# First per-layer embedding computed by token: factors on ScalarE, normalised rows turned back by products

## The chip, the cores and the metric

The kernel runs on one core of one Trainium2 chip. The metric is device time in microseconds (us) of one launch, the median of several runs; lower is better. The core's engines are TensorE (PE: matrix products; PEld: its weight loads), VectorE (DVE), ScalarE (ACT), GpSimd (POOL) and SyncE (SP, which here only issues weight loads).

## The reference

One sequence of 256 tokens with 1024 channels passes a first block (token mixer and a convolutional feed-forward part) and then a second block of two layers. Each layer of the second block is a mixer (a short convolution in layer 0, differential attention in layer 1), a feed-forward part and a per-layer embedding. Only the embedding of layer 0 and what touches it matters here:

```
def per_layer_embed(x, p_i, g_pre, w_gate, w_proj, g_post):
    gate = sigmoid(rms_norm(x, g_pre) @ w_gate)          # 256x1024 @ 1024x1024
    return rms_norm(gate * (p_i @ w_proj), g_post)       # 256x256 @ 256x1024
x = x + per_layer_embed(x, p[0], ...)                    # layer 0, then layer 1:
k, v = split(rms_norm(x, g_kv) @ w_kv);  q = rms_norm(x, g_pre_mix[1]) @ w_q
```

rms_norm divides each token by the root of the mean of its squares over the 1024 channels. All is float32.

## The kernel before, in words

**Layout.** The state x lies channel-major: eight chunks of 128 channels (partitions) by 256 tokens. To keep float32 accuracy with the fast product format, each operand is split into a high part (rounded) and a low part (the rest), and each product is done three times: high x high, low x high, high x low. Weights stream through a ring of three slots in blocks of 128x2048: SP loads a block into raw, ScalarE rounds it to w_hi (`split`, `ahead`, line 1662), VectorE subtracts to get w_lo (L2473), TensorE uses it and counts it in block_used. SP loads block n when the low part of block n-3 is done; ScalarE may round block n when TensorE has used block n-3.

**Order.** Each engine has one instruction queue, written out by hand; engines wait for each other on semaphores. Blocks n to n+3 below are the gate's four blocks, n+4 and n+5 the first two of attention (keys).

**Layer 0's embedding, by channel** (`ffn_and_ple`, L1475, on TensorE; L2257 on ScalarE; L3353 on VectorE). The projection p @ w_proj is done in two halves: the first half early, in `first_post` (L773), while the norm of the mixer's result is awaited; the second half (`late_proj`) when the feed-forward part ends, with the mean of its squares (`mean_of_y`) between. Both go by `proj_rows`, with channels as output partitions. The gate product x @ w_gate follows as x's chunks are updated (`high`, `part`, `channel_rows`): two blocks by parts, then the third whole, then `mean_of_x` (the mean of x's squares, from VectorE's sum folded at L2505), then the fourth, each bank of PSUM counted in bank_summed as it is finished. VectorE multiplies each bank by x's factor (L3382, L3384), ScalarE takes the sigmoid in place (L2281), VectorE multiplies by the projection (L3390, L3392), ScalarE squares (L2335), VectorE squares the last two (L3403), TensorE sums the squares over channels against ones (`mean_of_products`, L796) and fills with eight products of zeros (`keep_busy`, L708), ScalarE makes the factor (`rstd_y`, L1847), and VectorE scales, adds to x and makes attention's first operand (`add_post`, `led_chunks`, L3080). The first two chunks' high parts are made ahead of x's update (`early`, L3087).

**Layer 1's embedding, by token** (`last_layer`, L809; `last_products`, L2294 and L3424). Here tokens are the output partitions: bank b holds tokens 128 t to 128 t + 127 (t = b // 2) and half the channels (b % 2). x's factor is then one number a partition, so that ScalarE applies it as the scale of the sigmoid (L2302), squares with the sum over channels read as a by-product (L2311), and no mean on TensorE is needed for the products. The last bank is done in two halves (`last_quarter`, `half_sigmoid`). The mean of x's squares by token (`mean_by_token`, L891) stands inside the fourth block's second quarter. GpSimd makes factors by a power (L556, L558) for x and for the first tile; ScalarE makes the second tile's by Ln and Exp (L2329, L2330).

**Behind the embedding** the attention blocks start: `columns_by_chunk(5, ...)` (L615) does the first two key blocks chunk by chunk of x, 96 products, as the chunks' high and low parts come; the low part of the second block's weights is wanted from chunk 1 on (`second`, L627).

Of the kernel before, what the change touches and what calls it, by code (L numbers as in the profile page):

```python
# [16 lines left out]
P = 128  # L17
TOK = 256
# [91 lines left out]
SUMS_OF_ROW = [3, 3, 4, 4, 3, 4, 4, 5]  # L110
LED = (3, 5, 6)
SIX_FIRST = (6, 0, 1, 2, 3, 4, 5, 7)
SQUARES_OF_POST = [5, 5, 3, 5, 5, 4]
SUMS_OF_POST = [2, 2, 0, 2, 2, 4]
POST_BANK = (5, 4, 4, 5, 4)
GATE_BANK = (5, 0, 1, 2)
LAST_GATE_BANK = (6, 0, 1, 2)
TURN_BANK = (3, 5, 6, 7)
LAST_HALF_BANK = (2, 4)

# [6 lines left out]
def build(nc, weights, small_in, x_in, masks_in, ident_in, channel_in, row_in, w_gk_in, p_in, table_in,  # L127
# [4 lines left out]
    with ExitStack() as ctx:  # L132
# [311 lines left out]
        token_ms, minus_half = att_stat[1][:, 0:4], att_stat[1][:, 4:8]  # L444

# [67 lines left out]
        def _(pool):  # L513
# [34 lines left out]
            pool.dma_start(p_tok, p_in[1]).then_inc(sem("p_loaded"), 16)  # L548
            pool.wait_ge(sem("logits_read"), 8)
# [8 lines left out]
            pool.tensor_tensor(norm_r[:, 0:1], norm_bias[:, 0:1], minus_half[:, 0:1], ALU.pow).then_inc(sem("y_rstd"), 1)  # L558
# [3 lines left out]
        def _(pe):  # L562
# [52 lines left out]
            def columns_by_chunk(p, n0, banks, operand):  # L615
# [5 lines left out]
                if p in LED:  # L621
                    order = high[0:4] + low[0:1] + high[4:5] + low[1:4] + high[5:6] + low[4:6] + high[6:7] + low[6:7] + high[7:8] + low[7:8]
                for k, lo in order:
                    pe.wait_ge(lo_chunk if lo else hi_chunk, chunk_at(p, k) if lo else hi_at(p, k))
                    for j, bank in enumerate(banks):
                        slot = (n0 + j) % RING
                        second = j == 1 and k == 0 and not lo  # L627
                        if k == 0 and j == 0 and not lo:
                            block_ready(n0)
                        elif second:  # L630
                            pe.wait_ge(hi_ready, n0 + 2)
                        elif k == 1 and j == 0 and not lo:
                            pe.wait_ge(lo_ready, n0 + 2)
                            for f in range(2):
                                add(PS[:, banks[1], f * TOK:(f + 1) * TOK], w_lo[:, (n0 + 1) % RING, f * P:f * P + P], a_hi[:, 0, :])
# [72 lines left out]
            def keep_busy(n, bank):  # L708

                for _ in range(n):  # L710
                    add(PS[:, bank, :], zeros_r[:, 0:P], zeros_r[:, :], True, True)
# [35 lines left out]
            def proj_rows(layer, c, kk, w, first):  # L747


                o = PS[:, 6 + c // 2 % 2, (c % 2) * TOK:(c % 2 + 1) * TOK]  # L750
                ws_hi, ws_lo = w[0][:, kk, (c % 4) * P:(c % 4 + 1) * P], w[1][:, kk, (c % 4) * P:(c % 4 + 1) * P]
                p_hi, p_lo = p_parts(layer)
                add(o, ws_hi, p_hi[:, kk, :], first and kk == 0)
                add(o, ws_hi, p_lo[:, kk, :])
# [3000 lines left out]
```

## Time and profile before

| | |
|---|---|
| median of 3 runs | 1010.14 us (1009.93 to 1010.57) |
| the profiled execution | 1009.94 us, span 1008.1 us |
| granted TensorE clock, mean | 0.998 |
| TensorE busy | 997.1 us |
| VectorE busy | 848.4 us |
| ScalarE busy | 620.5 us |
| GpSimd busy | 9.5 us |

A timeline row tells the start in us from the span's start, the time of the row, the engine, the line of the kernel, the operation with output<-inputs, shape and count, and in square brackets the engine's idle time before it and who ended it. Rows of products have modelled ends: the time from one row's start to the next is what a product takes of the queue. A float32 product that is not in the fast format makes two records.

### The profile page before, as it was taken

The numbers are of one execution on the slowest core, as the hardware profiler recorded it, in microseconds if no ns is written. First come the engines' busy times: TensorE is split into PE (matmuls) and PEld (weight loads), VectorE is DVE, ScalarE is ACT, GpSimd is POOL, SyncE is SP. The second block draws the span as 40 slices with busy tenths as digits, with TensorE's granted clock in tenths as the row PEclk, the third lists the DMA queues.
The fourth block names the chain that finished last, engine by engine and source line by source line (L and its number), as shares of the span: only waits on it lengthen the run. The fifth ranks groups of instructions, "written<-read, shape, count | busy, mean of one in ns | idle before, by whom it ended". The sixth has DMA issues, their size and how long they took to land.

```text
span 1008.1 us, 20874 instructions
## 1 busy us (share of the span) xinstructions
PE 997.1 (99%) x8362; PEld 936.5 (93%) x8362; DVE 848.4 (84%) x1226; ACT 620.5 (62%) x858; POOL 9.5 (1%) x21
## 2 busy tenths in 40 slices
PE   8999999999999999999999999999999999999997
PEld 7999999999999998899999999999999999999996
DVE  5974896899988878879999888899776899988887
ACT  6754565657565655466666555775677676555575
POOL 0000001000000000001000000000000000000000
PEclk9999999999999999999999999999999999999999
DMA  9533315455655545566566554444444355655541
GB/s 330 179 124 97 126 44 201 165 192 187 208 190 184 196 143 204 180 235 210 199 209 209 174 203 171 165 165 170 165 147 152 126 204 205 212 178 196 184 150 42
DMA packets 26786, 177.04 MB, mean 176 GB/s; under 512 B 3261, under 2 KB 3541, under 8 KB 6368
## 3 DMA queue, kind: packets, MB, share of 16 engines
q1 hardware_dynamic: 25616, 171.31, 49.2%
q0 software_dynamic: 1104, 4.78, 1.6%
q8 instruction: 50, 0.82, 0.3%
q14 instruction: 16, 0.13, 0.0%
HBM read 175.02 MB, written 2.63 MB: 176 GB/s over the span
## 4 chain that ended last, share of the span: by engine, by line
PE 91%; DVE 4%; DMA 2%; ACT 2%; issue 1%; SPq 0%; DVEq 0%
PE PS L613 78%; PE PS L564 12%; DMA arena<-masks_in 1%; DVE w_lo L2473 1%; DMA raw<-weights 1%; DVE arena L2614 1%; DVE h_store L2486 0%; PE PS L1567 0%; DVE x L3158 0%; ACT w_hi L1662 0%; DVE arena L3390 0%; DVE arena L3152 0%; PE PS L935 0%; PE PS L903 0%; ACT arena L2043 0%
## 5 line engine op out<-in xcount | busy, mean ns | idle before, releaser
L613 PE MATMUL PS<-h_store,w_hi 128*128 128x256 f32 (+1 forms) x1840 | 475.5, 338 | 1.4 <-DVE w_lo L2528 1.2
L2473 DVE TENSOR_TENSOR w_lo<-raw,w_hi 128x2048 fp32r<-128x2048 f32 x152 | 347.9, 2290 | 50.6 <-ACT w_hi L1662 45.5
L613 PE MATMUL PS<-h_store,w_lo 128*128 128x256 f32 (+1 forms) x1400 | 365.4, 281 | 0.1
L1662 ACT ACTIVATE w_hi<-raw 128x2048 fp32r<-128x2048 f32 x154 | 294.2, 1911 | 82.6 <-PE PS L613 70.2
L613 PEld LDWEIGHTS PS<-h_store,w_hi 128*128 128x128 f32 x1840 | 303.6, 187 | 40.6 <-DVE w_lo L2528 1.7
L613 PEld LDWEIGHTS PS<-h_store,w_lo 128*128 128x128 f32 (+1 forms) x1400 | 253.2, 188 | 0.5 <-DVE h_store L3087 0.3
L613 PE MATMUL PS<-act_hi,w_hi 128*128 128x256 f32 x688 | 191.1, 280 | 0.2 <-DVE act_hi L3087 0.2
L613 PE MATMUL PS<-act_hi,w_lo 128*128 128x256 f32 x688 | 190.7, 279 | 0.1
L613 PE MATMUL PS<-act_lo,w_hi 128*128 128x256 f32 x688 | 187.6, 279 | 0.0
L613 PEld LDWEIGHTS PS<-act_hi,w_hi 128*128 128x128 f32 x688 | 129.3, 188 | 1.6 <-DVE act_hi L3087 0.6
L613 PEld LDWEIGHTS PS<-act_hi,w_lo 128*128 128x128 f32 x688 | 129.3, 188 | 0.3 <-DVE act_hi L3087 0.3
L613 PEld LDWEIGHTS PS<-act_lo,w_hi 128*128 128x128 f32 x688 | 127.5, 188 | 0.0
L2156 ACT ACTIVATE arena<-PS 128x512 f32<-128x512 f32 x51 | 30.2, 592 | 88.1 <-PE PS L613 88.1
L2148 ACT ACTIVATE arena<-arena,channel 128x256 f32<-128x256 f32 x132 | 63.6, 530 | 13.6 <-DVE arena L3235 12.4
L613 PE MATMUL PS<-w_hi,h_store 128*128 128x256 f32 (+1 forms) x368 | 71.3, 301 | 0.0
L3212 DVE SCALAR_TENSOR_TENSOR arena<-arena,channel 128x254 f32<-128x254 f32 x132 | 57.9, 480 | 7.6 <-DVE arena L3208 0.3
L613 PEld LDWEIGHTS PS<-w_hi,h_store 128*128 128x128 f32 x368 | 56.2, 188 | 2.9 <-ACT w_hi L1776 0.4
L3208 DVE SCALAR_TENSOR_TENSOR arena<-arena,channel 128x255 f32<-128x255 f32 x132 | 57.7, 479 | 1.0 <-ACT arena L2148 0.9
L3233 DVE TENSOR_TENSOR arena<-PS,arena 128x512 f32<-128x512 f32 x51 | 35.0, 686 | 20.9 <-ACT arena L2156 20.9
L613 PE MATMUL PS<-w_lo,h_store 128*128 128x256 f32 (+1 forms) x184 | 45.8, 296 | 0.4 <-DVE w_lo L2473 0.4
L564 PE MATMUL PS<-h_store,w_hi 128*128 128x256 f32 x256 | 45.4, 279 | 0.0
L564 PE MATMUL PS<-arena 64*64 64x64 f32 (+8 forms) x1356 | 41.5, 224 | 0.0
(405 smaller groups left out, 1147.1 us busy)
## 6 DMA issues: line engine op xcount, KB each, us to landing
raw<-weights SPq DMA_DIRECT2D x155, 1024.0 KB, 5.0
raw<-weights SPq DMA_DIRECT2D x12, 256.0 KB, 4.0
arena<-masks_in SPq DMA_DIRECT2D x1, 1600.0 KB, 12.2
bias_by_key<-bias_by_distance POOLq DMA_DIRECT2D x1, 1536.0 KB, 8.5
x<-x_in SPq DMA_DIRECT2D x4, 256.0 KB, 4.4
raw<-weights SPq DMA_DIRECT2D x2, 512.0 KB, 8.3
arena<-weights POOLq DMA_DIRECT2D x2, 512.0 KB, 6.1
arena<-bias_by_key POOLq DMA_DIRECT2D x1, 1024.0 KB, 6.6
```

The costliest lines, as they stand in the source:

```text
L564: return pe.matmul(o, lhs, rhs, start=start, stop=stop)
L613: return pe.matmul(o, lhs, rhs, start=start, stop=stop, skip_group_check=True)
L1662: act.activation(w_hi[:, slot, :], raw[:, slot, :], ACT.Copy).then_inc(hi_ready, 1)
L2148: ins = act.activation(dst[:, c, :], src[:, c, :], ACT.Identity, scale=w, bias=b)
L2156: act.activation(low, PS[:, bank:bank + 2, TOK:512], ACT.Copy).then_inc(sem("low_copied"), 1)
L2473: tt(w_lo[:, slot, :], raw[:, slot, :], w_hi[:, slot, :].bitcast(F), ALU.subtract).then_inc(lo_ready, 1)
L2614: mark(stt(dst, PS[:, bank_of_block(n), f * TOK:(f + 1) * TOK - d], ch("gdn_conv", (3 - d) * 6 + 2 * s + f), dst, ALU.mult, ALU.add))
L3208: stt(y[:, c, 1:TOK], src[:, c, 0:TOK - 1], channel[:, bass.ds(col(1) + c, 1)], y[:, c, 1:TOK], ALU.mult, ALU.add).then_inc(ready[0], 1)
L3212: ins = stt(y[:, c, 2:TOK], src[:, c, 0:TOK - 2], channel[:, bass.ds(col(0) + c, 1)], y[:, c, 2:TOK], ALU.mult, ALU.add)
L3233: tt(z, PS[:, bank:bank + 2, 0:TOK], low, ALU.add).then_inc(sem("parts_added"), 1)
```

## The change

Layer 0's embedding is computed like layer 1's, by token:

- TensorE: the projection goes by `proj_tokens` in both layers, and `last_layer` becomes `embedding(layer, p, q)` for both. In layer 0 the mean by token stands behind the third gate block's first quarter, and the last bank's products of the third block are done with that block (`halves(4, 6)`), so that only those of the fourth remain at the end. `mean_of_products` and `proj_rows` go. Six products of zeros follow, then the new part: the products g, which lie by token, must come back by channel. `scale_and_turn` multiplies a 128x128 piece of g with a diagonal matrix of the token factors (`rate_rows`), which scales and turns it in one float32 product: eight for the first tile of tokens, then four of the second, and the last four between the first attention products (`turn_second_tile`).
- ScalarE: `gated_products` for both layers (token factor as the sigmoid's scale); two more copies of the late projection; at the end the second tile's factor and its diagonal matrix (a scaled copy of ident).
- GpSimd: the first tile's factor by a power and its diagonal matrix (a product of ident with a column).
- VectorE: no reading with a factor, no scaling; `add_turned` updates x straight from the turned banks. The low part of the second attention block is made in two halves, the second within `add_turned`; `columns_by_chunk(5, ...)` wants it four chunks later (`late = 4`). In both layers the first tile's mean stands before the third product.

```diff
@@ GpSimd
+            link(pool.memset(minus_half, -0.5))
+            pool.wait_ge(sem("y_sum"), y_sum(2, 1))
+            link(pool.tensor_tensor(norm_r[:, 0:1], norm_bias[:, 0:1], minus_half[:, 0:1], ALU.pow))
+            pool.tensor_scalar(rate_rows[0], ident[:, :], norm_r[:, 0:1], None, ALU.mult).then_inc(sem("first_rate"), 1)
             pool.wait_ge(sem("logits_read"), 8)
@@ TensorE, columns_by_chunk
+                late = 4 if p == 5 else 1
                 for k, lo in order:
+                    if p == 5 and k in (1, 2) and not lo:
+                        turn_second_tile(range(2 * k + 2, 2 * k + 4))
...
-                        second = j == 1 and k == 0 and not lo
+                        second = j == 1 and k < late and not lo
@@ TensorE, first_post
-                proj_rows(0, 0, 0, early_proj, True)
+                proj_tokens(0, 0, 6, 0, early_proj)
                 mean_of_y(0)
-                proj_rows(0, 0, 1, early_proj, True)
-                proj_rows(0, 1, 0, early_proj, False)
+                proj_tokens(0, 0, 6, 1, early_proj).then_inc(sem("proj_half"), 1)
+                proj_tokens(0, 1, 7, 0, early_proj)
                 biases_by_head()
...
+                proj_tokens(0, 1, 7, 1, early_proj).then_inc(sem("proj_half"), 1)
@@ TensorE, embedding
+            def scale_and_turn(c, t):
+
+                return mm(turned(c)[:, t * P:(t + 1) * P], by_quarter[:, 2 * t + c // 4, (c % 4) * P:(c % 4 + 1) * P], rate_rows[t])
+
+            def turn_second_tile(chunks):
+
+                for c in chunks:
+                    done = scale_and_turn(c, 1)
+                    if c in (0, 1, 3, 5, 7):
+                        done.then_inc(sem("y_scaled"), 1)
...
                 for b in range(3):
                     gate(2, b)
+                    if layer == 0 and b == 0:
+                        mean_by_token()
+                if layer == 0:
+                    halves(4, 6, False).then_inc(block_used, 1)
...
                 gate(3, 0).then_inc(bank_summed, 1)
-                gate(3, 1, mean_by_token).then_inc(bank_summed, 1)
+                gate(3, 1, mean_by_token if layer else None).then_inc(bank_summed, 1)
                 gate(3, 2).then_inc(bank_summed, 1)
...
+                halves(4 if layer else 6, KC, True)
+                if layer == 0:
+                    keep_busy(6, 5).then_inc(block_used, 1)
+                    pe.wait_ge(sem("first_rate"), 1)
+                    pe.wait_ge(sem("gate_sigmoid"), 3)
+                    for c in range(KC):
+                        last = scale_and_turn(c, 0)
+                    last.then_inc(sem("y_ms"), 1)
+                    pe.wait_ge(sem("y_rstd"), q + 2)
+                    turn_second_tile(range(4))
@@ ScalarE, gated_products
                 gate_sigmoid(0)
                 gate_sigmoid(1)
                 square(0)
-                gate_sigmoid(2)
-                square(1)
+                if layer:
+                    gate_sigmoid(2)
+                    square(1)
+                else:
+                    square(1)
+                    gate_sigmoid(2)
                 half_sigmoid(0)
                 square(2)
...
                 half_sigmoid(1)
                 act.preload_act_table_set(TABLES)
...
                 link(act.activation(r, sum_of_squares[:, 4:5], ACT.Ln, bias=norm_bias[:, 1:2]))
-                act.activation(r, r, ACT.Exp, scale=-0.5).then_inc(sem("y_rstd"), 1)
+                if layer:
+                    act.activation(r, r, ACT.Exp, scale=-0.5).then_inc(sem("y_rstd"), 1)
+                else:
+                    link(act.activation(r, r, ACT.Exp, scale=-0.5))
+                    act.activation(rate_rows[1], ident[:, :], ACT.Copy, scale=r).then_inc(sem("y_rstd"), 1)
@@ VectorE, add_turned (new)
+                early(0, first_gain, first_x)
+                early(1, second_gain, second_x)
+                update(2)
+                update(3)
+                update(0)
+                update(4)
+                lo(0, 3)
+                between()
+                update(1)
...
@@ VectorE, ffn_and_ple
+                gated_products(layer, z, q + 1)
                 if layer == 0:
...
+                    half_lo(n + 5, 0)
+                    add_turned(p + 1, q + 1, lambda: half_lo(n + 5, 1))
```

## Rows read from the trace of the kernel before

**Rows 1.** The page, part 1: busy time of each engine, share of the span, instructions.

```profile
PE 997.1 (99%) x8362; PEld 936.5 (93%) x8362; DVE 848.4 (84%) x1226; ACT 620.5 (62%) x858; POOL 9.5 (1%) x21
```

**Rows 2.** Windows: engines' busy us (instructions), granted clock, DMA share and GB/s.

```profile
640.00:668.00 28.00, 28.00 (x230) 27.57 (x230) 26.64 (x42) 19.94 (x31) 0.00 (x0) 1.00 0.53 184
668.00:674.00 6.00, 5.63 (x24) 3.99 (x23) 5.79 (x12) 5.06 (x8) 0.00 (x0) 1.00 0.14 33
```

**Rows 3.** Timeline of TensorE around the first embedding.

```profile
640.17 0.28 PE L613 MATMUL PS<-first_p_hi,w_hi 128*128 128x256 f32 x1
640.29 0.28 PE L613 MATMUL PS<-first_p_lo,w_hi 128*128 128x256 f32 x1
...
667.52 2.05 PE L613 MATMUL PS<-xn,ones 128*128 128x256 f32 x8
...
673.78 0.39 PE L613 MATMUL PS<-act_hi,w_hi 128*128 128x256 f32 x1 [0.16 <-DVE act_hi L3087]
...
685.55 2.04 PE L613 MATMUL PS<-h_store,w_hi 128*128 128x256 f32 x16
```

**Rows 4.** Timeline of TensorE in the last embedding.

```profile
972.29 0.39 PE L613 MATMUL PS<-w_hi,act_hi 128*128 128x512 f32 x1
...
989.12 0.61 PE L613 MATMUL PS<-w_hi,h_store 128*128 128x512 f32 x2
...
990.48 0.61 PE L613 MATMUL PS<-w_hi,h_store 128*128 128x512 f32 x2
```

**Rows 5.** Timeline of TensorE, first product of the first feed-forward part of the second block.

```profile
456.03 0.28 PE L613 MATMUL PS<-h_store,w_hi 128*128 128x256 f32 x1
```

**Rows 6.** Timeline of VectorE: the fold of the sum of squares.

```profile
657.77 0.43 DVE L2505 TENSOR_TENSOR arena<-arena 128x256 f32<-128x256 f32 x1
```

**Rows 7.** Timeline of ScalarE in the last embedding.

```profile
995.82 1.26 ACT L2302 ACTIVATE arena<-PS,arena 128x512 f32<-128x512 f32 x2 [4.57 <-POOL arena L556]
...
1000.17 0.62 ACT L2311 ACTIVATE xn<-arena 128x512 f32<-128x512 f32 x1
...
1000.83 0.42 ACT L2323 ACTIVATE xn<-arena 128x256 f32<-128x256 f32 x1
...
1001.25 0.46 ACT L2306 ACTIVATE arena<-PS,arena 128x256 f32<-128x256 f32 x1
1001.73 1.28 ACT L2326 ACT_TABLE_LOAD   x1
1003.02 0.29 ACT L2329 ACTIVATE arena<-arena 128x1 f32<-128x1 f32 x1
1003.35 0.20 ACT L2330 ACTIVATE arena<-arena 128x1 f32<-128x1 f32 x1
```

**Rows 8.** Timeline of VectorE in the last embedding.

```profile
999.05 0.69 DVE L3431 TENSOR_TENSOR arena<-arena 128x512 f32<-128x512 f32 x1
...
1001.74 0.43 DVE L3435 TENSOR_TENSOR arena<-arena 128x256 f32<-128x256 f32 x1
```

**Rows 9.** Timeline of TensorE: float32 products of 256 and 128 columns.

```profile
723.65 1.47 PE L613 MATMUL PS<-arena 128*128 128x256 f32 x8
```

**Rows 10.** Timeline of VectorE: the first attention operand.

```profile
673.24 0.48 DVE L3087 SCALAR_TENSOR_TENSOR act_hi<-arena 128x256 fp32r<-128x256 f32 x1
```

**Rows 11.** Groups by line of GpSimd: operation, shape, count, busy us, mean ns, idle time.

```profile
L556 POOL TENSOR_TENSOR arena<-arena 128x4 f32<-128x4 f32 x1 | 1.1, 1052 | 224.8 <-DVE arena L3458 224.8
...
L558 POOL TENSOR_TENSOR arena<-arena 128x1 f32<-128x1 f32 x1 | 0.9, 926 | 4.2 <-DVE arena L3448 4.2
...
L523 POOL MEMSET ones<- 128x128 f32 x1 | 0.2, 209 | 0.0
```

**Rows 12.** The page's DMA issues (part 6), and ScalarE's timeline at the fifth attention block.

```profile
raw<-weights SPq DMA_DIRECT2D x155, 1024.0 KB, 5.0
...
691.13 1.90 ACT L1662 ACTIVATE w_hi<-raw 128x2048 fp32r<-128x2048 f32 x1
```

**Rows 13.** Instructions of line 2281: the sigmoid in place, without a factor.

```profile
L2281 ACT ACTIVATE arena<-arena x5: 399/632/632, 665.2 to 668.6; 128x512 f32<-128x512 f32 x3, 128x256 f32<-128x256 f32 x2
```

More of the change, by code:

```diff
@@ L444, in build, with turned @@
         token_ms, minus_half = att_stat[1][:, 0:4], att_stat[1][:, 4:8]
+        rate_rows = [r_x2[:, t * P:(t + 1) * P] for t in range(TT)]
+        def turned(c):
+            bank, at = TURNED_AT[c]
+            return PS[:, bank, at:at + TOK]
         def hi_at(p, c):
@@ L1491, in ffn_and_ple @@
-                last.then_inc(block_used, 1)
-                n = STEP[f"ple_gate{layer}"]
-                def part(j, k, cs, a, w, first=False):
-                    for c in cs:
-                        at = k % 2 * D + c * P
-                        o = PS[:, GATE_BANK[c // 2], (c % 2) * TOK:(c % 2 + 1) * TOK]
-                        last = add(o, w[:, (n + j) % RING, at:at + P], a[:, k, :], first and c % 2 == 0)
-                    return last
-                def high(k, cs, first=False):
-                    part(0, k, cs, h_hi, w_hi, first)
-                    part(0, k, cs, h_hi, w_lo)
@@ L2275, in ffn_and_ple, with gated_products @@
+                for b in (1, 3):
+                    act.activation(by_quarter[:, b, :], PS[:, TURN_BANK[b], :], ACT.Copy).then_inc(sem("proj_copied"), 1)
+                if layer == 0:
+                    ahead(n + 2)
+                    first_operand(5, 2)
+                    rstd_x(p + 1, 3, r_x[:, TOK:TOK + 4])
                 act.preload_act_table_set("sigmoid_and_others")
+                gated_products(layer, p, q + 1)
+            def gated_products(layer, p, q):
                 z = (s_gate, hidden, y_gate, y_up)
-                def sigmoid(part):
-                    act.wait_ge(sem("ple_z"), part + 1)
-                    v = flat(z[part]) if part < 3 else z[3][:, part - 3, :]
-                    act.activation(v, v, ACT.Sigmoid).then_inc(sem("gate_sigmoid"), 1)
@@ L2301, in gate_sigmoid @@
                     at = TOK + 2 * (b // 2)
-                    act.activation(flat(z[b]), PS[:, LAST_GATE_BANK[b], :], ACT.Sigmoid, scale=r_x[:, at:at + 1]).then_inc(sem("gate_sigmoid"), 1)
+                    act.activation(flat(z[b]), PS[:, GATE_BANK[b], :], ACT.Sigmoid, scale=r_x[:, at:at + 1]).then_inc(sem("gate_sigmoid"), 1)
                 def half_sigmoid(half):
-                    act.wait_ge(bank_summed, bank_sum(7, 4 + half))
+                    act.wait_ge(bank_summed, bank_sum(row, 4 + half))
```

316 lines of the change are left out of this document (112 added, 204 removed).

## The prediction, made before the changed kernel was built

> **What bounds the kernel now.** I read the page first, then the windows around the first embedding, then each engine's timeline there. TensorE is busy 99% of the span [rows 1]. So an edit is worth what it does to TensorE's own order, and other engines count only where TensorE waits for them. The windows show where it does [rows 2]: from 640 to 668 us it never waits, and from 668 to 674 us it has 5.63 busy us of 6, part of which is keep_busy, eight products of zeros. The fixed points are in its timeline [rows 3]: the embedding starts at 640.17, the last gate product's slot ends at 667.52, the first attention product starts at 673.78, and the 96 products of the first two attention blocks end at 685.55. The six us from 667.52 to 673.78 hold a serial chain: read, sigmoid, product, squares, their mean on TensorE, norm on ScalarE, scaling, first operand. From 673.78 on, 96 products at the 0.117 us between neighbouring rows, 640.17 and 640.29, would take 11.25 us; they take 11.77.
>
> The last embedding already has the form that the first is given, so much of the new stage has rows to read. It starts at 972.29, its third gate block's first quarter ends at 989.12, and a quarter block (six products of 512 columns) takes 990.48 - 989.12 = 1.36 us [rows 4].
>
> **The projection and the first two gate blocks.** On the new time line the third block's first quarter ends at 640.17 + (989.12 - 972.29) = 657.00; fewer, wider products are in that figure. The early projection in front of the first feed-forward part goes from 24 products of 256 columns to 12 of 512, the same columns. Its mean starts 3 x 0.117 = 0.35 us later, behind three wide products, and so does the norm; but the wide products behind the mean still last until about 456.03, where TensorE turns to the next operand now [rows 5]. I take 0, and up to 0.35 for the range.
>
> **The mean behind the first quarter: a wait that the change adds.** The mean needs VectorE's folded sum of squares: folded at 657.77 for 0.43 us, so there at 658.20 and not earlier, with no idle time shown before it [rows 6]. TensorE comes at 657.00 and stands until about 658.26: 1.26 us, with all other gate products queued behind. Today the mean stands behind the whole third block, past 661, and waits for nothing. This is the largest single loss. Then come the mean by token (two float32 products of at most 0.22 each, 0.4), five quarter blocks at 1.36, and 24 half products of 256 columns at 0.12, half of them before the fourth block, half behind it: 2.88. The sum is 658.26 + 0.4 + 6.80 + 2.88 = 668.34, against 667.52: the gates end 0.8 later.
>
> **ScalarE and VectorE up to the second tile's factor.** Two copies out of PSUM are added to ScalarE before the token factors; it is idle for 8 us between 640 and 668 [rows 2], and the sigmoids can't start before the first bank sum at 664.2. They cost 0. The second bank sum comes at 658.26 + 0.4 + 2.72 + 1.44 + 2.72 = 665.54, and ScalarE follows some 0.2 behind a product's slot, at 665.75. From there on ScalarE and VectorE alternate, by the last embedding's rows [rows 7, 8]. Sigmoid 1 takes 1.26/2 = 0.63, VectorE's product 0.69, two semaphores 0.1: square 1 starts at 667.17. A square with its sum read takes 1000.83 - 1000.17 = 0.66: sigmoid 2 at 667.83. Again 0.63, 0.69 and 0.1: square 2 at 669.25, the half square at 669.91. It takes 0.42, the last half sigmoid 0.48, the table load 1.29, Ln 0.33, Exp 0.20: Ln starts at 672.10, the factor is there at 672.63. VectorE's half product, 0.43, its reduction and mean, as short, lie beside the table load. So ScalarE's queue sets the end, and the gates' last sums (668.34) are no longer on it. The new row of factors is a copy of 128x128 with no row: between Exp's 0.20 of one column and the 0.48 of 256 columns. I take 0.35, in the middle, so that TensorE starts the second tile at 673.05.
>
> **Turned products.** These are float32 products with 128 columns. Eight records of such work (two products of 256 and two of 128 columns, so six times 128) take 1.47 us with their tail [rows 9]: 0.22 each without it. The first is there 0.45 after its start, at 673.5. VectorE's first operand takes 0.48 [rows 10], and the first attention product starts at about 674.1, against 673.78. So squares of VectorE, eight means of products and a scaling go, and the copy, the turn and the added wait take their place.
>
> **The first tile and GpSimd.** Square 1 ends near 667.9; VectorE's mean and GpSimd's power, 0.93 [rows 11], bring it to 669.1. Then GpSimd multiplies ident by the factor, 128x128, which no row shows. The nearest row is the 128x128 memset, 0.21; the steepest reading is the power's slope, (1.05 - 0.93)/3 = 0.042 us a column, 5.4 us for 128. I take 0.4: a plain product is nearer the memset. TensorE fills until about 669.7, then turns eight chunks in 8 x 0.22 = 1.8 us, to 671.5, and waits 1.5 us for the second tile anyway. So the GpSimd product costs nothing below about 2.1 us. Queued behind its wait are only the loads of the next projection and of the last gains, which wait for the end of the attention heads anyway. The Trainium skill ("GPSIMD Engine Reference", section 3.1) gives an elementwise operation there 1.8 to 2.6 cycles an element and two software hops; an estimate from that page is 0.2 to 0.5 us, and no run here shows it yet.
>
> **The attention blocks.** The last four chunks of the second tile are turned between attention products: 4 x 0.22 = 0.88 us of TensorE, which has 0.52 us of waits to give there. 674.1 + 0.1 + 11.25 + 0.88 = 686.3 against 685.55. VectorE loses its scalings. The low half of the second attention block moves from before the norm into two pieces; the order of products now lets four chunks pass before it is wanted: 24 high and 4 low products and four turns behind 674.2, at 678.4. VectorE gets there after seven operations of some 0.4 and the piece's own 1.2, at 677.6. SP's next load waits for that low part and starts about 5 us later; it lands in 5.0 us, at about 682.7, and ScalarE comes to round it only at 691.13, behind x's factor [rows 12]. Hidden; without that cover it would cost 1 to 3 us.
>
> **Sum.** 686.3 - 685.55 = 0.75 later, and behind it TensorE is as full as before. In the last embedding only VectorE's mean moves ahead of a product, with slack on both sides: 0. The profiled execution took 1009.94 us with a span of 1008.1; the median of the runs is 1010.14, 0.2 above it. I forecast 1010.14 + 0.75 = 1010.9 us.
>
> The token factor as ScalarE's scale: a sigmoid of 512 columns in place, without a factor, takes 0.632 us [rows 13]; with a column of factors it takes 0.63 [rows 7]. The sum takes the factor as free. The Trainium skill ("ScalarE: Activation LUTs", on what ACT_TABLE_LOAD and ACTIVATE cost) says that each [128,1] pointer operand adds about 93 ns, which speaks against this change: by that page the chain's sigmoids and squares would be up to 0.4 us longer, and the time 1011.3. The trace does not agree, unless reading PSUM directly gives it back.
>
> **The rivals.** (a) Faster: TensorE doesn't wait at the mean, as VectorE folds earlier once nothing is read into it, and the turns run at the 0.117 of a product of 256 columns. For it: ScalarE's chain then starts 1.26 earlier. Against: VectorE has no idle time before the fold, and float32 is slower in [rows 9]. It gives 1010.9 - 1.26 - 0.4 - 0.8 (the chunks' waits all covered) = 1008.4 at most. Chance 0.12. (b) Slower: GpSimd's 128x128 product. From 2.1 us on it decides. At the slope's 5.4 the first tile's factors are there at 674.5, turned by 676.3, and the second tile starts then instead of at 673.05: 3.2 us, 1014.1. For it: no row has the form; against: the memset. Chance 0.1. (c) Slower by the clock: TensorE would stand 1.3 us at the mean and 1.5 us before the second tile. The granted clock is 1.00, its 2.4 GHz level, in both windows [rows 2], also where it waits now. At 1.2 GHz every us of its work costs another; three such us give 1014. Chance 0.05. (d) The chain is longer by 1 to 1.8 us than rows of another stage say (more semaphores, a slower copy): 1012.3. Chance 0.1. (e) The forecast, 1009.2 to 1012.0: 0.63.
>
> **How the numbers follow.** A measurement of this kernel tells about 0.2%, 2.0 us, from no change. Faster by more needs most of (a): 0.1. Slower by more takes (b), (c) and half of (d): 0.2. The rest is within: 0.7. The range goes down to the wait absent and cheap turns, 1008.6, and up to (d)'s end, 1012.7; the far ends of (b) and (c) are left out.
>
> **What the profile would show.** Right: TensorE idle for over 1 us before the mean by token, released by VectorE's fold; the gates ending 0.8 later; the row of factors on ScalarE releasing the second tile near 673; the first attention product near 674.1; its blocks ending near 686.3. Wrong: no wait at the mean, turns under 0.15 us, a GpSimd product over 2 us, a granted clock below 1.00 after 657, or the first feed-forward part starting late.

## The result and the profile after

| | before | after |
|---|---|---|
| median, same chip | 1010.17 us (22 runs) | 1011.81 us (22 runs) |
| ratio to before | | 1.0014, 95% interval 1.0008 to 1.0019 |
| profiled execution | 1009.94 us, span 1008.1 | 1013.26 us, span 1011.2 |

The forecast was 1010.9 us: no change that a measurement tells, some 0.75 us slower by its sum. The medians differ by 1.64 us, the ratio of the runs is 1.0014, or 1.4 us (0.8 to 1.9). That lies inside the range and within the 0.2%. But with 22 runs of each kernel the interval is clear of 1: the slowdown is small and real, and about twice the forecast one.

The profiled execution of after is the longest of its 22. So I compare stages, not ends, each from a fixed row to a fixed row of TensorE:

| stage, us | before | after |
|---|---|---|
| first product of the first embedding, to the end of the 96 attention products | 640.17 to 685.55: 45.38 | 641.84 to 688.41: 46.57 |
| from there to the last embedding's first product | 286.74 | 286.58 |
| last embedding, to the end of the span | 972.29 to 1008.1: 35.81 | 974.99 to 1011.2: 36.21 |

The first embedding adds 1.19 us. The last seems to add 0.40, but the span's end is printed to 0.1 us only. Counted to the start of VectorE's last three operations it is 0.36 (these rows are shown below). The stretch between takes 0.16 less. Together that is 1.4 of the 3.1 us by which the spans differ; the other 1.67 lie before the first embedding. 1.58 of them are there already at the first early projection product (450.81 before, 452.39 after), where the change has done nothing yet; the early projection and its mean take 5.31 instead of 5.22. In line numbers, before's L613 is L626 after, L2505 (the fold) is L2447, L2302 (the sigmoid with a factor) is L2241, L3431 (VectorE's product) is L3376, L3448 (VectorE's mean) is L3393. Rows of L577 with 128 columns are the turned products. In a run whose edit adds or removes lines, the numbers shift by a few.

The page's part 1 of after, one line; before's is in [rows 1]:

```profile
PE 996.3 (99%) x8282; PEld 931.4 (92%) x8282; DVE 843.8 (83%) x1217; ACT 621.3 (61%) x866; POOL 11.2 (1%) x24
```

VectorE lost 4.6 us and TensorE 0.8 of busy time, and nothing came of it: TensorE's time without work in the span grew from 11.0 us (1008.1 - 997.1) to 14.9 (1011.2 - 996.3). The windows of after around the embedding, to be read beside [rows 2]:

```profile
641.00:669.00 28.00, 26.90 (x139) 22.30 (x138) 25.08 (x39) 19.89 (x32) 0.00 (x0) 1.00 0.50 175
669.00:676.00 7.00, 5.92 (x42) 5.11 (x41) 3.93 (x10) 6.37 (x16) 1.53 (x2) 1.00 0.14 56
```

TensorE stands 1.10 us in the first and 1.08 in the second. The granted clock stays at 1.00, its 2.4 GHz level. Its timeline shows where; it answers to [rows 3]:

```profile
641.84 0.39 PE L626 MATMUL PS<-w_hi,first_p_hi 128*128 128x512 f32 x1
...
658.53 0.40 PE L626 MATMUL PS<-w_lo,h_store 128*128 128x512 f32 x1
660.03 0.61 PE L626 MATMUL PS<-ones,arena 128*128 128x2 f32 x4 [1.10 <-DVE arena L2447]
660.50 0.71 PE L626 MATMUL PS<-w_hi,h_store 128*128 128x512 f32 x2
...
670.43 1.55 PE L626 MATMUL PS<-zeros_r 128*128 128x512 f32 x6
672.07 2.05 PE L577 MATMUL PS<-arena 128*128 128x128 f32 x16
675.12 1.16 PE L577 MATMUL PS<-arena 128*128 128x128 f32 x8 [1.01 <-ACT arena L2277]
676.19 0.39 PE L626 MATMUL PS<-act_hi,w_hi 128*128 128x256 f32 x1
...
677.00 0.61 PE L577 MATMUL PS<-arena 128*128 128x128 f32 x4
...
688.41 2.03 PE L626 MATMUL PS<-h_store,w_hi 128*128 128x256 f32 x16
```

The wait at the mean is there, released by VectorE's fold. The bracket says 1.10, but a product takes 0.23 of the queue and not its row's 0.40: the slot of the product at 658.53 ends at 658.76, and the queue lost 660.03 - 658.76 = 1.27. The second wait is for ScalarE's row of factors. VectorE in front of the mean, and then ScalarE's chain with its end (they answer to [rows 6] and [rows 7]):

```profile
658.83 0.69 DVE L2442 TENSOR_TENSOR arena<-arena,xn 128x512 f32<-128x512 f32 x1
659.55 0.42 DVE L2447 TENSOR_TENSOR arena<-arena 128x256 f32<-128x256 f32 x1
```

```profile
667.81 0.69 ACT L2241 ACTIVATE arena<-PS,arena 128x512 f32<-128x512 f32 x1 [0.65 <-PE PS L626]
...
669.25 0.63 ACT L2250 ACTIVATE xn<-arena 128x512 f32<-128x512 f32 x1
...
669.88 0.67 ACT L2241 ACTIVATE arena<-PS,arena 128x512 f32<-128x512 f32 x1
...
671.31 0.63 ACT L2250 ACTIVATE xn<-arena 128x512 f32<-128x512 f32 x1 [0.39 <-DVE arena L3376]
...
671.94 0.40 ACT L2266 ACTIVATE xn<-arena 128x256 f32<-128x256 f32 x1
...
672.34 0.45 ACT L2245 ACTIVATE arena<-PS,arena 128x256 f32<-128x256 f32 x1
672.81 1.28 ACT L2269 ACT_TABLE_LOAD   x1
674.11 0.29 ACT L2272 ACTIVATE arena<-arena 128x1 f32<-128x1 f32 x1
...
674.67 0.40 ACT L2277 ACTIVATE arena<-ident,arena 128x128 f32<-128x128 f32 x1
```

The half sigmoid at 672.34 has had its sum since the gates' end at 670.43. It is late because of ScalarE's own queue. GpSimd, which answers to [rows 11]:

```profile
670.38 0.57 POOL L559 TENSOR_TENSOR arena<-arena 128x1 f32<-128x1 f32 x1 [200.80 <-DVE arena L3393]
671.06 0.95 POOL L560 TENSOR_SCALAR arena<-ident,arena 128x128 f32<-128x128 f32 x1
```

And VectorE in the last embedding, to be read beside [rows 8]:

```profile
1001.99 0.21 DVE L3393 TENSOR_SCALAR arena<-arena 128x1 f32<-128x1 f32 x1 [0.17 <-ACT xn L2250]
1002.12 0.68 DVE L3376 TENSOR_TENSOR arena<-arena 128x512 f32<-128x512 f32 x1
```

Before, the third product started at 999.05, 26.76 us behind that embedding's first product on TensorE (972.29); now it starts at 1002.12, 27.13 behind (974.99). The mean stands in front of it and waits 0.17 for ScalarE's second square. VectorE's last three operations, first before, then after:

```profile
1003.59 2.06 DVE L3454 SCALAR_TENSOR_TENSOR arena<-arena,PS 128x512 f32<-128x512 f32 x3 [0.15 <-ACT arena L2330]
```

```profile
1006.65 2.06 DVE L3399 SCALAR_TENSOR_TENSOR arena<-arena,PS 128x512 f32<-128x512 f32 x3 [0.16 <-ACT arena L2274]
```

They start 1003.59 - 972.29 = 31.30 us and 1006.65 - 974.99 = 31.66 us behind the embedding's first product: 0.36 later.

### The profile page after: what moved, and what is told of

Read it like the earlier page. It is cut to its first block, busy times and chain, and to the rows that moved or that the text cites. A ratio compares the mean times of both kernels' runs of the same rounds, so it can differ in the third digit from the quotient of the medians.

```text
span 1011.2 us, 20720 instructions
## 1 busy us (share of the span) xinstructions
PE 996.3 (99%) x8282; PEld 931.4 (92%) x8282; DVE 843.8 (83%) x1217; ACT 621.3 (61%) x866; POOL 11.2 (1%) x24
## 4 chain that ended last, share of the span: by engine, by line
PE 91%; DVE 3%; ACT 2%; DMA 2%; issue 1%; SPq 0%; DVEq 0%; POOL 0%; POOLq 0%
PE PS L626 78%; PE PS L577 12%; DMA arena<-masks_in 1%; DVE w_lo L2415 1%; DMA raw<-weights 1%; DVE arena L2556 1%; PE PS L1524 0%; DVE h_store L2428 0%; DVE x L3140 0%; ACT xn L2250 0%; DVE arena L3376 0%; ACT L2269 0%; ACT arena L2241 0%; ACT w_hi L1619 0%; DVE arena L3134 0%
## 5 line engine op out<-in xcount | busy, mean ns | idle before, releaser
L626 PE MATMUL PS<-h_store,w_hi 128*128 128x512 f32 (+1 forms) x1712 | 455.0, 342 | 2.3 <-DVE w_lo L2470 2.0
L626 PE MATMUL PS<-h_store,w_lo 128*128 128x256 f32 (+1 forms) x1336 | 351.5, 281 | 0.3 <-DVE w_lo L2415 0.2
L626 PEld LDWEIGHTS PS<-h_store,w_hi 128*128 128x128 f32 x1712 | 285.7, 187 | 41.4 <-DVE w_lo L2470 2.5
L626 PEld LDWEIGHTS PS<-h_store,w_lo 128*128 128x128 f32 (+1 forms) x1336 | 242.8, 188 | 0.9 <-DVE w_lo L2415 0.4
L626 PE MATMUL PS<-act_hi,w_hi 128*128 128x256 f32 x688 | 190.6, 280 | 0.0
L626 PE MATMUL PS<-act_hi,w_lo 128*128 128x256 f32 x688 | 190.0, 279 | 0.0
L626 PE MATMUL PS<-act_lo,w_hi 128*128 128x256 f32 x688 | 187.5, 279 | 0.0
L626 PEld LDWEIGHTS PS<-act_hi,w_hi 128*128 128x128 f32 x688 | 129.0, 188 | 1.1
L626 PEld LDWEIGHTS PS<-act_hi,w_lo 128*128 128x128 f32 x688 | 128.9, 188 | 0.0
L626 PEld LDWEIGHTS PS<-act_lo,w_hi 128*128 128x128 f32 x688 | 127.4, 188 | 0.0
L626 PE MATMUL PS<-w_hi,h_store 128*128 128x256 f32 (+1 forms) x448 | 90.8, 310 | 0.5 <-issue 0.5
L626 PEld LDWEIGHTS PS<-w_hi,h_store 128*128 128x128 f32 x448 | 69.8, 188 | 5.4 <-ACT w_hi L1733 0.8
L626 PE MATMUL PS<-w_lo,h_store 128*128 128x256 f32 (+1 forms) x224 | 58.1, 306 | 0.6 <-DVE w_lo L2415 0.6
L577 PE MATMUL PS<-arena 64*64 64x64 f32 (+9 forms) x1388 | 45.9, 226 | 1.1 <-ACT arena L2277 1.0
L577 PEld LDWEIGHTS PS<-arena 64*64 64x64 f32 (+6 forms) x1388 | 38.1, 130 | 9.3 <-issue 1.9
```

The source lines that it names most:

```text
L577: return pe.matmul(o, lhs, rhs, start=start, stop=stop)
L626: return pe.matmul(o, lhs, rhs, start=start, stop=stop, skip_group_check=True)
```

## The experiments

All are edits of the changed kernel. "Stage" is the first row of the table above (after: 46.57 us), "last" its third (36.21). Both are read in the profiled execution. Runs of one group share a chip and the runs of the kernel before, to which the ratios are.

**First group: is it the wait at the mean, ScalarE's queue, or both?** The changed kernel itself:

> The changed kernel as it is, beside the kernel before on the chip that the next three runs share. Forecast's theory: 0.75 us over before by its sum, 1.2 by the embedding's stretch in the trace (46.57 us from its first product to the end of the 96 attention products, against 45.38): 1.0007 to 1.0015 of before. A rival puts the difference down to the executions: then 1.000, and the sign is open.

Measured: 1012.08 us against 1010.14, ratio 1.0014 (1.0005 to 1.0023); stage 46.58, last 36.26. The difference repeats, and so do both stages, to 0.05 us, although this profiled execution took 1015.75 us. Its extra time is elsewhere, a wait of 1.6 us of TensorE in the feed-forward part among it. The stages are far steadier than the ends.

**The mean one quarter later:**

```diff
-                    if layer == 0 and b == 0:
+                    if layer == 0 and b == 1:
                         mean_by_token()
```

> First embedding's mean by token moved behind the second quarter of the third gate block instead of the first. Forecast's theory: VectorE's fold was ready 1.10 us after TensorE came, and a quarter lasts 1.40, so the wait goes whole and nothing else gets later: sigmoids, token factors and attention blocks all come 1.1 us earlier, the 46.57 us of the embedding and its attention blocks become 45.5, and the time falls 1.1 us below after_again (0.9989 of it). Rival A: the serial chain on ScalarE, VectorE and GpSimd behind the gates sets the second tile's start by itself: the wait only moves to the place ahead of the turns, 0 to 0.3 us gained. Rival B: the fold isn't what came last (the wait has two releasers, the fold and the scaled rows): a wait of some size stays at the mean.

Measured: 1010.67 us, 1.0005 (0.9996 to 1.0014), 1.41 below after_again by the medians. Stage 45.21, 1.36 shorter. TensorE's timeline has no wait at the mean, and the later wait for ScalarE is as long as it was:

```profile
660.28 0.39 PE L626 MATMUL PS<-w_lo,h_store 128*128 128x512 f32 x1
660.51 0.50 PE L626 MATMUL PS<-ones,arena 128*128 128x2 f32 x4
660.87 0.72 PE L626 MATMUL PS<-w_hi,h_store 128*128 128x512 f32 x2
...
674.10 1.16 PE L577 MATMUL PS<-arena 128*128 128x128 f32 x8 [1.01 <-ACT arena L2277]
```

The gain is the 1.27 us of the queue plus 0.11 of the mean, which takes 0.36 (660.51 to 660.87) right behind other products and took 0.47 (660.03 to 660.50) after standing still. My 1.1 had been read from the bracket. Rivals A and B fall: ScalarE's chain starts with the gates and moves with them, and the fold was what came last.

**ScalarE's end of the chain:**

(Semaphore counts at the ends of lines and the conditions on the layer are left out.)

```diff
@@ ScalarE, gated_products (layer 0)
                 half_sigmoid(0)
+                half_sigmoid(1)
                 square(2)
-                act.wait_ge(sem("ple_product"), product + 4)
-                act.activation(sq4[:, 3, 0:TOK], prod[:, 6, :], ACT.Square, scale=D ** -0.5, accum_out=sum_of_squares[:, 3:4])
-                half_sigmoid(1)
@@ VectorE, gated_products (layer 0)
                 half_product(0)
+                dve.wait_ge(sem("ple_product"), 4)
+                u = prod[:, 6, :]
+                dve.tensor_tensor_reduce(sq4[:, 3, 0:TOK], u, u, 1.0 / D, 0.0, ALU.mult, ALU.add, sum_of_squares[:, 3:4])
```

> The mean stays behind the first quarter. In the first embedding ScalarE takes the last half sigmoid ahead of the third square, and the half square of the last bank goes to VectorE as a product with its sum. Theory that ScalarE's queue, not the gates' last sums, sets the second tile's factor: the queue is shorter by 0.40 (half square) and the last half sigmoid (now 672.34, with its sum there since 670.43) moves ahead of a square that waits for VectorE; Ln starts near 673.3 instead of 674.11, the second tile is turned from 674.25 instead of 675.12, bounded there by the first tile's turns, and the time falls 0.85 us below after_again. Rival: VectorE's half product, product with sum and mean become the end: 0.3 us or less gained. Rival: the order before attention isn't what bounds the attention products, which wait for VectorE's operands: 0.

Measured: 1011.05 us, 1.0007 (0.9998 to 1.0016), 1.03 below after_again; stage 45.79, 0.78 shorter. ScalarE and then TensorE:

```profile
669.44 0.83 ACT L2245 ACTIVATE arena<-PS,arena 128x256 f32<-128x256 f32 x2
670.30 0.63 ACT L2250 ACTIVATE xn<-arena 128x512 f32<-128x512 f32 x1
670.84 0.19 ACT L2250 ACTIVATION_READ_ACCUMULATOR xn<-arena 128x1 f32 x1
671.04 1.28 ACT L2272 ACT_TABLE_LOAD   x1
```

```profile
671.05 2.05 PE L577 MATMUL PS<-arena 128*128 128x128 f32 x16
673.35 1.16 PE L577 MATMUL PS<-arena 128*128 128x128 f32 x8 [0.25 <-ACT arena L2280]
```

The table load comes right behind the square, and the wait ahead of the second tile goes from 1.01 to 0.25. So ScalarE's queue did set that wait, and not the gates' last sums. The forecast had said so.

**Both:**

> Both edits together. Theory: they are in series, TensorE's wait ahead of ScalarE's queue, so they add up: 1.1 + 0.85 = 1.95 us below after_again, 0.998 of it, and some 0.5 us below before. Rival: with the wait gone the first tile's turns, which wait for GpSimd's power and product (1.5 us behind the first mean), set the second tile's start: 1.2 to 1.5 us in all, level with before.

Measured: 1009.22 us, 0.9993 (0.9984 to 1.0002); stage 44.46, 2.11 shorter, and 1.36 + 0.78 = 2.14 was the sum of the two. They are in series. The interval holds 1, so this run alone doesn't show a kernel faster than the one before; the stages do show it. GpSimd doesn't take over: the wait ahead of the second tile is again 0.25, for ScalarE.

**Second group: the last embedding, the turns between products, the two halves.** The first edit, in layer 1 alone:

```diff
-                mean(0, 0, 1, 2)
                 product(2)
+                mean(0, 0, 1, 2)
```

> The changed kernel, with VectorE's mean in the last embedding put back behind the third product, as before. In the traces the last embedding lasts 36.21 to 36.26 us in the changed kernel and its three variants, 35.81 in the kernel before. Theory (against the forecast's step, which gave it 0): the mean now waits 0.17 us for ScalarE's second square and then takes its own time, and the product behind it, the half product, the half square, the table load, Ln and the last results all come 0.37 to 0.40 us later: 35.83 again, and 0.4 us off the time (0.9996 of the changed kernel). Rival: the stage is longer by its products on TensorE or by the load of gains, and the order on VectorE had slack: 36.2 stays.

Measured: 1011.40 us, 1.0008 (0.9999 to 1.0017). The stage stays at 46.54, the last embedding goes from 36.21 to 35.92. VectorE:

```profile
999.56 0.69 DVE L3376 TENSOR_TENSOR arena<-arena 128x512 f32<-128x512 f32 x1
1000.16 0.21 DVE L3393 TENSOR_SCALAR arena<-arena 128x1 f32<-128x1 f32 x1
```

The product starts 999.56 - 972.78 = 26.78 us behind the embedding's first product, as before (26.76), and the mean behind it waits for nothing. The last three operations follow:

```profile
1004.09 2.06 DVE L3399 SCALAR_TENSOR_TENSOR arena<-arena,PS 128x512 f32<-128x512 f32 x3 [0.15 <-ACT arena L2274]
```

They start 1004.09 - 972.78 = 31.31 us behind the embedding's first product, against 31.66 in the changed kernel and 31.30 before. The rival (TensorE's products, the gains' load) would have left 31.66. So the order on VectorE costs the whole 0.36 us. That 35.92 still stands over before's 35.81 is the rounding of the span's end.

> q2_tail and last_mean_back together. Theory: two stages that don't overlap add up: first embedding and its attention blocks 44.46 us (45.38 before), last embedding 35.83 (35.81 before): 0.9 us below before, 0.9991 of it, some 2.5 below the changed kernel. Rival: q2_tail's 0.9993 was the luck of its executions: 0.9997 or more.

Measured: 1009.44 us, 0.9990 (0.9981 to 0.9999); stage 44.44, last 35.89. This version is faster than both kernels, by 0.1% against before, and the rival falls, though the interval only just excludes 1.

**No turns between the attention products:**

```diff
-                    turn_second_tile(range(4))
+                    turn_second_tile(range(8))
...
-                    if p == 5 and k in (1, 2) and not lo:
-                        turn_second_tile(range(2 * k + 2, 2 * k + 4))
```

> The changed kernel with all eight chunks of the second tile turned ahead of attention and none between its products. The forecast took 0.22 us a turn, wherever it stands. TensorE has no gap in the trace from the first attention product (676.19) to the end of the 96 (688.41), so nothing is hidden between the products: theory, 0 (at most 0.2 either way; the first product comes 0.9 to 1.0 later, the blocks end where they did). Rival 1: the turns between cover TensorE's waits for VectorE's operands; without them some 0.5 us of waits come back, and the time rises 0.5. Rival 2: they interrupt the pipeline (a switch of kind each time): 0.3 to 0.5 faster without.

Measured: 1011.23 us, 1.0004 (0.9995 to 1.0013); stage 46.37, 0.20 shorter.

```profile
673.67 2.05 PE L577 MATMUL PS<-arena 128*128 128x128 f32 x16 [1.00 <-ACT arena L2275]
675.48 0.36 PE L626 MATMUL PS<-act_hi,w_hi 128*128 128x256 f32 x1
```

Eight turns take 1.81 us of the queue, 0.23 each, and the first attention product follows them without a wait. In the changed kernel four turns take 0.91 and the product comes 1.07 behind the first turn (675.12 to 676.19). The 0.16 between is a stop for VectorE's first operand that the other four turns would have covered. Behind that product the blocks take 12.22 us with four turns and 11.29 without, 0.23 a turn again. So turns between products hide nothing, for no wait is left there to hide, and rival 1 falls. The 0.2 us that the order costs isn't rival 2's either: it is the uncovered first operand.

**The low half in one piece, ahead:**

```diff
-                late = 4 if p == 5 else 1
+                late = 1
...
                     half_lo(n + 5, 0)
-                    add_turned(p + 1, q + 1, lambda: half_lo(n + 5, 1))
+                    half_lo(n + 5, 1)
+                    add_turned(p + 1, q + 1, lambda: None)
```

> The changed kernel with the low half of the second attention block made in one go ahead of the first operand, as in the kernel before, and its products in the order of before. VectorE makes its first half from 673.77 to 674.98 beside Ln and the factor; the second half would hold it to 676.2, and the first operand, now started at 675.65, comes some 0.55 later. Theory: 0.3 to 0.6 us slower. Rival: the piece between the updates (at 678.44, 1.2 us) holds up the operands of the later chunks by as much now: 0.

Measured: 1011.97 us, 1.0013 (1.0004 to 1.0022); stage 46.94, 0.37 longer, as the theory had it. TensorE now waits for the first operand:

```profile
675.28 0.39 PE L626 MATMUL PS<-act_hi,w_hi 128*128 128x256 f32 x1 [0.28 <-DVE act_hi L3074]
```

This part of the change pays: by the stage it saves 0.4 us. The intervals of the times (this run's 1.0004 to 1.0022, the changed kernel's 1.0008 to 1.0019) are too wide to show it.

**Third group: the forecast's unknown prices.** GpSimd's product, four times (the added line stands three times over):

```diff
+            link(pool.tensor_scalar(rate_rows[0], ident[:, :], norm_r[:, 0:1], None, ALU.mult))
             pool.tensor_scalar(rate_rows[0], ident[:, :], norm_r[:, 0:1], None, ALU.mult).then_inc(sem("first_rate"), 1)
```

> The changed kernel with GpSimd's 128x128 product of ident and the first tile's factor done four times, one after the other, into the same row of factors (the same numbers; the first tile is released by the fourth). This measures the term that the forecast gave 0.4 us and called free below about 2.1. One product takes 0.95 us in the trace. Forecast's rule with the measured product: 4 x 0.95 and three semaphores, some 4.1 us, is 2.0 above the cover, so the first tile's turns start near 3.1 us later, the second tile's follow them without a wait 2.0 us later than now, and the time rises 2.0 us (1.0034 of before; first embedding and its attention blocks 48.6 us instead of 46.57). Rival: GpSimd's product is on the chain already, as the first tile's turns start 0.06 us behind it: every extra one costs its whole length, 3.1 us, 49.7.

Measured: 1015.42 us (4 runs), 1.0054 (1.0040 to 1.0069); stage 48.64, 2.07 longer. GpSimd and TensorE:

```profile
670.14 0.95 POOL L560 TENSOR_SCALAR arena<-ident,arena 128x128 f32<-128x128 f32 x1
671.18 0.60 POOL L561 TENSOR_SCALAR arena<-ident,arena 128x128 f32<-128x128 f32 x1
671.88 0.84 POOL L562 TENSOR_SCALAR arena<-ident,arena 128x128 f32<-128x128 f32 x1
672.81 1.64 POOL L563 TENSOR_SCALAR arena<-ident,arena 128x128 f32<-128x128 f32 x1
```

```profile
674.51 2.94 PE L580 MATMUL PS<-arena 128*128 128x128 f32 x24 [3.43 <-POOL arena L563]
```

The four take 4.31 us. The first tile's turns start 33.57 us behind the embedding's first product (640.94 here) instead of 30.23: 3.34 later, the whole of what was added. The stage shows 2.07 of it, and 1.27 is hidden. The cover was the second tile's wait. In the changed kernel the first tile's turns end at 30.23 + 1.81 = 32.04 (eight turns take 1.81, see turns_before) and the second tile starts at 33.28, so the wait cost the queue 1.24; its bracket says 1.01. So the product is free up to 0.95 + 1.24 = 2.19 us, and the forecast had said about 2.1: the rival falls, the threshold is right. The time did not come out as expected: 1.0054 for 1.0034, with an interval that leaves 1.0034 out. The median is 3.6 us over the changed kernel's 1011.8, with only four runs. The 1.5 us beyond the stage I have not traced, and the profiled execution (1014.40) doesn't show them.

**No filler:**

```diff
-                    keep_busy(6, 5).then_inc(block_used, 1)
+                    keep_busy(1, 5).then_inc(block_used, 1)
```

> The changed kernel with one product of zeros ahead of the first tile's turns instead of six; TensorE then stands still for some 1.3 us there. The forecast's rival (c) was that standing still costs the clock. Theory: the granted clock stays at 1.00 (2.4 GHz) and the turns, which wait for GpSimd and ScalarE, start when they did: 0 us (first embedding and its attention blocks 46.6). Rival: the clock falls to 0.5 (1.2 GHz) behind the gap and products take twice as long until it rises: over 1 us slower, and a granted clock under 1.00 in the windows from 670 on.

Measured: 1011.58 us, 1.0013 (1.0004 to 1.0022); stage 46.55, unchanged. TensorE's row and the windows from the gap on:

```profile
669.84 2.05 PE L577 MATMUL PS<-arena 128*128 128x128 f32 x16 [1.24 <-POOL arena L560]
```

```profile
668.50:670.00 1.50, 0.26 (x2) 0.16 (x2) 0.89 (x2) 1.11 (x4) 1.18 (x2) 1.00 0.07 22
670.00:676.00 6.00, 4.99 (x41) 4.70 (x42) 4.69 (x12) 5.83 (x11) 0.00 (x0) 1.00 0.00 0
```

TensorE stands still 1.24 us there, and the clock stays at its 2.4 GHz level; the row of turns takes 2.05 as before. The filler bought nothing here. In pool_x4 TensorE stood 3.43 us in one piece, and the granted clock was 1.00 in the windows 668 to 672, 672 to 676 and 676 to 680 us.

**No factor in the sigmoids:**

```diff
-  PS[:, GATE_BANK[b], :], ACT.Sigmoid, scale=r_x[:, at:at + 1])
+  PS[:, GATE_BANK[b], :], ACT.Sigmoid)
```

> The changed kernel with the token's factor left out of the sigmoids of 512 columns of both embeddings (a constant scale in place of the column of factors; the output differs from the reference by it). This measures what a column of factors costs ScalarE: those sigmoids take 0.67 to 0.69 us with it. The forecast took it as free. By the Trainium skill (ScalarE: Activation LUTs, on the cost of ACTIVATE) a [128,1] pointer operand would add some 93 ns. Without the column: 0.58 to 0.60 us by that page, 0.67 to 0.69 if it is free and reading PSUM makes the difference to the 0.632 of the kernel before. In the first case the stage is some 0.1 to 0.2 us shorter, as two or three sigmoids stand in the chain.

One run, 1011.02 us, so the time says nothing here; stage 46.39, 0.18 shorter, last 35.99, 0.22 shorter. ScalarE's group of this line, first in the changed kernel, then here (the numbers behind the bar are the busy time and the mean ns of one):

```profile
L2241 ACT ACTIVATE arena<-PS,arena 128x512 f32<-128x512 f32 x6 | 4.0, 681 | 7.5 <-POOL arena L568 4.6 <-PE PS L626 3.0
```

```profile
L2241 ACT ACTIVATE arena<-PS 128x512 f32<-128x512 f32 x6 | 3.5, 593 | 7.6 <-POOL arena L568 4.5 <-PE PS L626 3.0
```

The column of factors costs 681 - 593 = 88 ns a sigmoid. The Trainium skill ("ScalarE: Activation LUTs", section "What ACT_TABLE_LOAD costs") gives some 93 ns, and this run agrees. The forecast set its own rows against that page and was misled twice. Its 0.63 us for a sigmoid with a factor is half of a row of 1.26 in which two records overlap; each of these records lasts 669 to 687 ns in the trace of before. And the in-place sigmoid of [rows 13] (632) differs in a second thing, it doesn't read PSUM. Without a factor it is 632 ns in place and 593 out of PSUM, 39 less, under half of the column's price.

**The best version:** q2_tail_back with the turns of turns_before.

> q2_tail_back with turns_before: the mean by token behind the second quarter, ScalarE's shorter tail, the last embedding's mean behind its product, and all eight chunks of the second tile turned ahead of attention. By the stages measured alone: 44.44 - 0.20 = 44.24 us for the first embedding and its attention blocks (before 45.38), 35.9 for the last (35.81), so 1.1 to 1.3 us below before: 0.9987 to 0.9990. Rival: with the chain shorter, the eight turns in a row hold up the first product where it doesn't wait for VectorE: 44.4, and 0.9990 to 0.9992.

Measured: 1009.25 us, 0.9988 (0.9980 to 0.9997); stage 44.22, last 35.82. Before had 45.38 and 35.81. The stages add up as expected, and the rival's 44.4 is not reached. The eight turns of the second tile stand in one row:

```profile
671.78 2.05 PE L577 MATMUL PS<-arena 128*128 128x128 f32 x16 [0.25 <-ACT arena L2278]
```

## Why the prediction was right, and where it was off

By the forecast's own steps, each time counted from the embedding's first product (640.17 there, 641.84 in the trace of after):

| step | forecast | after | edit that showed it |
|---|---|---|---|
| TensorE comes to the mean | 16.83 | 16.92 | |
| wait for the fold ends | 18.09 | 18.19 | mean_q2 |
| sigmoid 1 | 25.58 | 25.97 | |
| sigmoid 2, behind square 1 | 27.66 | 28.04 | |
| Ln | 31.93 | 32.27 | tail_only |
| second tile starts | 32.88 | 33.28 | tail_only, pool_x4 |
| first attention product | 33.93 | 34.35 | turns_before, late1 |
| end of the blocks | 46.13 | 46.57 | turns_before |

- **The added wait** was forecast at 1.26 and cost 1.27 us of the queue. It is the largest single loss, as said, and taking it out gave it back whole. Rival (a), that it wouldn't be there, falls.
- **Sigmoid 1, off by 0.39**, and every later time by 0.34 to 0.44. The parts: wait 0.10, the mean 0.07 (0.47 for 0.4), the first two quarter blocks 0.17, the next two 0.08. The forecast took the quarter block's 1.36 from [rows 4]; here two took 2.89 and 2.80, 1.40 to 1.45 each. This is the term that was too small. Why these products go slower here than in the last embedding, at the same granted clock, stays open. From there to the second tile the sum held to 0.01 us.
- **Row of factors** on ScalarE: 0.35 forecast, 0.40 measured. **Turns:** 0.22 forecast, 0.23 measured. **GpSimd's product:** 0.4 forecast, 0.95 measured, over twice as much, and free all the same. The step that called it free below a threshold held: pool_x4 lost only what went over the threshold. By the Trainium skill ("GPSIMD Engine Reference", section 3.1) my estimate had been 0.2 to 0.5; this trace differs, and the measurement decides. Rival (b) fell on the price.
- **Turns between attention products** were said to cost 0.88 of TensorE, and took 0.93. What the forecast missed is that four turns in front leave the first operand uncovered for 0.16.
- **Rival (c)**, the clock: 1.00 throughout, also in no_filler. It falls. **Rival (d)**, the chain longer than the rows say: longer by 0.4, not by 1 to 1.8.
- **The step that failed:** "In the last embedding only VectorE's mean moves ahead of a product, with slack on both sides: 0". It cost 0.36. The mean there waits for ScalarE's second square (0.17), the product stands behind it, and product, half product, half square, table load, Ln and the last results follow one by one. I had seen that VectorE had idle time later on ([rows 8]) and not that the product was what ScalarE waited for next. last_mean_back gave all of it back. In layer 0 the same order costs nothing: there the mean (670.01 for 0.21) lies in idle time, as the product behind it (670.59) still waits 0.36 for ScalarE's sigmoid. No run tried the other order in layer 0.
- **The column of factors** was taken as free; it costs 0.088 us a sigmoid, about 0.2 us in each embedding. The rows of [rows 7] had it inside already, so the sum did not suffer. What failed is the reading that the trace doesn't agree with the page: it compared half of a merged row with a single record.
- **The attention blocks:** the sum's terms behind the first product held, 12.20 forecast and 12.22 measured. The load released by the later low half cost nothing that shows: the stretch behind the blocks takes 286.58 us for 286.74.

The sum again with what was measured: 1.19 and 0.36, less 0.16 between the embeddings (286.58 for 286.74; the edited versions have 286.4 to 286.7, so this may be scatter), is 1.39 us. The runs gave 1.0014, 1.4 us. The forecast of 0.75 is about half of that: 0.44 us more lie in the first embedding, most of them in its pace, and 0.36 in the last embedding, which it had at nothing; the 0.16 go the other way. So the mechanism of the first embedding held, the wait and the chain with their sizes. That the time came out inside the stated range owes as much to the range, 1008.6 to 1012.7, which is wide against either error.

**Open:** why a quarter block takes 1.40 us in the first embedding and 1.36 in the last, and pool_x4's median.

## What to carry to other kernels

When a wait is added to the queue of the busiest engine, move the waiting instruction behind one more piece of work that doesn't need it: here, one quarter block further on, 1.4 us came back for one changed number. Before an order is changed in a second place "for free", ask what the instruction that now stands second releases on the other engine; idle time later in the queue is no slack for it. And where a short tail of small operations runs on one engine, look for the operation whose input has long been there: taking it forward, and giving one square to the neighbour, was worth 0.8 us.

## What the hardware showed that I had not expected

- GpSimd's 128x128 product of a matrix with a column took 0.95 or 0.96 us in eleven runs with one of them and 0.87 in the twelfth (no_factor), but 0.95, 0.60, 0.84 and 1.64 in a row of four alike; its power of one column took 0.57 here and 0.91 in the last embedding of the same trace.
- A wait costs TensorE's queue more than the bracket says, by the 0.17 us by which a row outlasts its slot, and the first small products behind it took 0.11 us more.
- A sigmoid of 512 columns that read PSUM took 39 ns less than one in place in SBUF (593 ns on average in no_factor, 632 in before, both without a factor).
- In the two profiled executions of the changed kernel the embeddings' stages agree to 0.05 us (46.57 and 46.58, 36.21 and 36.26), while the times differ by 2.5 us (1013.26 and 1015.75).
